# A fused decoder trunk: at the borders between sub-layers, VectorE's low-part split of the first row tile moves in front of the gate products of the second

## The reference

```
h = rmsnorm(x, g_pre) * (1 + scale) + shift      # scale, shift, gate come from a vector c
y = sublayer(h)                                   # products of h with weights
x = x + gate * rmsnorm(y, g_post)
```

## Time and profile before

| | us |
|---|---|
| median of 3 runs (878.6 to 879.68) | 879.16 |
| the profiled execution, its time | 878.76 |
| its span, first to last instruction | 877.0 |
| PE busy | 863.8 (99%) |
| PEld busy | 719.7 (82%) |
| DVE busy | 661.7 (75%) |
| ACT busy | 419.0 (48%) |
| POOL busy | 115.5 (13%) |
| mean granted TensorE clock | 0.991 |

### The profile page before, as it was taken

How to read it: one execution, slowest core, us unless ns; L and a number is a source line. 1 busy time by engine, 2 the same in 40 slices (tenths; PEclk the granted TensorE clock), 3 DMA queues, 4 the chain that set the end, 5 groups by cost and what they waited for, 6 DMA issues and landing times.

```text
span 877.0 us, 11703 instructions
## 1 busy us (share of the span) xinstructions
PE 863.8 (99%) x4259; PEld 719.7 (82%) x4259; DVE 661.7 (75%) x1170; ACT 419.0 (48%) x635; POOL 115.5 (13%) x103
## 2 busy tenths in 40 slices
PE   9999999999999999999999999999999999999996
PEld 8987888888877888888888778888887788888885
DVE  4688989898788676676488899888787855644844
ACT  4464655465545543443336555465554635434521
POOL 1610120301221040300321030030030100000300
PEclk8999999999999999999999999999999999999998
DMA  8886764767344878677445766566644374665511
GB/s 343 355 305 238 241 223 172 285 200 304 104 163 155 350 260 322 251 262 280 171 144 201 280 222 258 193 231 233 255 146 169 104 281 168 237 244 190 206 59 48
DMA packets 34362, 194.09 MB, mean 221 GB/s; under 512 B 4481, under 2 KB 4481, under 8 KB 16770
## 3 DMA queue, kind: packets, MB, share of 16 engines
q1 hardware_dynamic: 32978, 189.64, 58.7%
q0 software_dynamic: 1328, 3.71, 1.3%
HBM read 192.29 MB, written 1.05 MB: 220 GB/s over the span
## 4 chain that ended last, share of the span: by engine, by line
PE 90%; DVE 6%; DMA 2%; issue 1%; ACT 1%; SPq 0%; DVEq 0%; ACTq 0%
PE ps L1232 26%; PE ps L1234 26%; PE ps L1233 25%; PE ps L1283 5%; PE ps L1335 2%; PE ps L1372 2%; DMA wide_t<-ada_first 1%; DVE w_lo L845 1%; PE ps L1363 1%; PE ps L1357 1%; PE ps L1356 1%; PE ps L1355 1%; PE ps L1334 1%; PE ps L1317 1%; DVE pj L1081 1%
## 5 line engine op out<-in xcount | busy, mean ns | idle before, releaser
L845 DVE TENSOR_TENSOR w_lo<-raw,w_hi 128x2048 fp32r<-128x2048 f32 (+1 forms) x132 | 303.8, 2309 | 48.4 <-ACT w_hi L606 46.6
L1232 PE MATMUL ps<-w_hi,t_hi 128*128 128x512 f32 (+1 forms) x832 | 326.7, 393 | 2.0 <-DVE t_lo L1037 1.9
L1234 PE MATMUL ps<-w_hi,t_lo 128*128 128x512 f32 (+1 forms) x832 | 319.8, 384 | 0.0
L1233 PE MATMUL ps<-w_lo,t_hi 128*128 128x512 f32 (+1 forms) x832 | 319.1, 384 | 0.0
L606 ACT ACTIVATE w_hi<-raw 128x2048 fp32r<-128x2048 f32 (+1 forms) x132 | 249.8, 1895 | 13.6 <-PE ps L1234 9.2
L1232 PEld LDWEIGHTS ps<-w_hi,t_hi 128*128 128x128 f32 x832 | 157.3, 189 | 34.8 <-DVE t_lo L1037 3.3
L1234 PEld LDWEIGHTS ps<-w_hi,t_lo 128*128 128x128 f32 x832 | 157.1, 189 | 30.9
L1233 PEld LDWEIGHTS ps<-w_lo,t_hi 128*128 128x128 f32 x832 | 157.5, 189 | 28.5
L499 POOL PARTITION_ALL_REDUCE wide_t<-wide_t x10 | 64.2, 6422 | 586.9 <-DVE wide_t L863 586.9
L863 DVE SCALAR_TENSOR_TENSOR wide_t<-ada,cs,wide_t 128x1024 f32<-128x1024 f32 x80 | 102.3, 1279 | 0.8 <-DMA ada<-w_ada 0.5
L1232 PE MATMUL ps<-w_hi,m_hi 128*128 128x512 f32 x240 | 99.2, 414 | 0.2
(11 more groups left out here) (164 smaller groups left out, 793.7 us busy)
## 6 DMA issues: line engine op xcount, KB each, us to landing
raw<-w_stream SPq DMA_DIRECT2D x128, 1024.0 KB, 5.9
ada<-w_ada SPq DMA_DIRECT2D x80, 512.0 KB, 5.3
wide_t<-ada_first SPq DMA_DIRECT2D x5, 1024.0 KB, 8.4
wide_t<-gains POOLq DMA_DIRECT2D x7, 512.0 KB, 5.2
mixed<-ada_first SPq DMA_DIRECT2D x3, 1024.0 KB, 6.7
raw<-w_stream SPq DMA_DIRECT2D x4, 656.0 KB, 6.4
x<-x_in SPq DMA_DIRECT2D x1, 1024.0 KB, 5.1
out<-x SPq DMA_DIRECT2D x4, 256.0 KB, 2.0
```

Source lines behind the costliest of these rows:

```text
L845: nc.vector.tensor_tensor(w_lo[:, U % RING, 0:n], raw[:, U % RAW, 0:n], w_hi[:, U % RING, 0:n].bitcast(F32), ALU.subtract).then_inc(s_lo, 1)
L1232: nc.tensor.matmul(dst, hi, w_h, start=first, stop=False)
L1233: nc.tensor.matmul(dst, hi, w_l, start=False, stop=False)
L1234: return nc.tensor.matmul(dst, lo, w_h, start=False, stop=last)
```

## The change

In DVE's `border`, `h_lo(to, kind, 0)`, the two low-part subtractions of tile 0, is issued in front of `gated(l, mid, 1)`, the two gate products of tile 1, and no longer behind them. Four instructions at each of three borders change places; nothing is added or removed, and no other engine's program changes.

```diff
                     scaled(0)
                     dve.wait_ge(s_shift, 2 * l + (1 if mid else 2))
                     normed(l, mid, 0)
-                gated(l, mid, 1)
                 if more:
                     h_lo(to, kind, 0)
+                gated(l, mid, 1)
                 added(l, mid, 1)
                 if more:
                     scaled(1)
```

## The result

The changed kernel is slower: 885.08 us median of 13 runs (880.7 to 887.8) against 879.46 for the kernel before (13 runs, 877.68 to 882.65), ratio 1.0055 with a 95% interval of 1.0042 to 1.0069. The forecast was 882.4, a ratio of 1.0037, from +3.26 us. Measured are +5.6 us by the two medians and +4.8 by the ratio: direction right, size too small by 2.4 or 1.6 us. The profiled execution took 881.74 us, span 880.0, mean granted clock 0.995, so it stands near the low end of its kernel. That it is 3.3 us under the median is part of what had to be explained.

A forecast was written before the change was run, and what follows sets the result against it. PE, busy 99% of the span, was taken as the bound. Shifts of 0.97 + 1.33 + 0.96 = 3.26 us took the profiled 878.76 us to 882.02, and 0.40 more to the median gave 882.4 us; range 880.8 to 884.5.

The forecast's parts named there:

- The bound and the mechanism: At the borders: PE bounds the kernel, and tile 1's chain from DVE's `added` to PE has no slack.
- The shifts: Later start of `added(1)` on DVE, reaching PE in full: 0.97 us at A, 1.33 at B, 0.96 at C.
- Tile 0's gain: Border A: `t_lo` of tile 0 starts 0.39 us sooner, PE can use only 0.21, which lengthens its tile 1 wait.
- Border B as the worst one: Border B: gate products sit wholly in DVE's wait for `t_hi`; moving them gains tile 0 nothing and costs +1.33 us.
- The absorbed shift: Later stages: DMA or POOL's reductions set the pace, hiding up to half the shift; about +1.2 us, 880.4; chance 0.12.
- tile 0 decides: Borders A and C: tile 1's transposes are released early enough, only 0.21 us each comes back; -0.4 us, 878.8; chance 0.04.
- reordering: On DVE: gate products run while the subtraction ahead of them waits, so no effect; chance 0.03.
- The clock: PE's 3.2 us between tiles at A and C drops its clock: 884.1 us for one border, 885.7 for both; chance 0.17.
- 0.50 behind A or C: Sign of a wrong prediction: PE's clock rows show 0.50, that is 1.2 and not 2.4 GHz, after border A or C.

The follow-up runs named there:

- with fills: Changed kernel plus useless matmuls in PE's waits around tile 1's transposes at A and C (two of four runs also at B): pooled mean 883.29 us against 884.83.
- the second profile: Profile from a repeat of the changed kernel, word for word the same: 885.47 us median of 7 against 878.92 for the kernel before.
- the pure-delay run: Kernel before, old order, with useless DVE instructions in front of `added(1)`, two at A and C, three at B: 887.11 us median of 6, ratio 1.0096.
- the third profile of the changed kernel: Profile from another repeat of the changed kernel, nothing altered: 884.32 us median of 12 against 880.36 for the kernel before.

## Why the prediction was right, and what was mis-sized

**The bound and the mechanism.** Right. Tile 1's chain from `added(1)` to PE had no slack, and PE's start was moved by all of the delay; the delay alone does it too (+4.09 us of stretch with nothing moved). One piece of the evidence was misread: of the ten waits of weight loads for `normed`, four are tile 0's, the longest (0.73 and 0.71 us) among them; tile 1's six come to 1.5 us, the longest 0.38.

**The shifts.** Predicted 0.97, 1.33 and 0.96, sum 3.26; measured 1.01, 1.41 and 1.01, sum 3.43. The term that was too small is the step from the gate products to `added`: I took 0.04 us from the pair of dependent steps on SBUF, and it is 0.10 (259.41 + 1.28 to 260.79). DVE's idle of 0.72 us at A and the 1.35 us of the two subtractions were right to 0.01.

**Tile 0's gain.** I gave PE 0.21 us, from the bracket of its wait. The real matmuls start 2.89 us after `normed(0)` and not 3.27, so it was 0.38, which is the whole of `t_lo`'s 0.39: the shown end of the fills is later than the moment from which PE could start. As argued, it reached nothing.

**Border B as the worst one.** Right: the gate products lay wholly in a wait, and `t_lo` of tile 0 did not move.

**The absorbed shift, tile 0 decides, reordering.** None occurred; the distances between the stretches are unchanged to 0.13 us.

**The clock.** This is the term that was left out of the sum. I wrote "If it falls, 3.3 us at half speed lose 1.65 us" and gave it 0.17, with the full clock as the likeliest case. The price of a fall was nearly right (1.43 and 1.56 measured); the chance was not. The pooled 1.5 us between the changed kernel without and with fills would be, at 1.5 us a fall, about one in each execution, over two borders. That is an estimate: falls were seen in one profile of three, two of them, and none in the profile of the new order at A and C alone. The rows I had (2.0 us left the clock alone, 3.9 us did not) bracketed the new 3.2 us; seen from the result, about even odds for each border and an added term of some 1.5 us would have come closer: 3.43 + 1.5 gives 4.9, and 5.1 is measured. The prediction also named 0.50 behind A or C as a sign of being wrong; by that sign its clock failed in the second profile, and its chain did not.

**Slower by how much.** 885.08 lies 0.6 us above the upper end of the stated range; the ratio times the given median of before (1.0055 x 879.16 = 884.0) lies inside it, near the end that allowed for one fall of the clock.

What stays open: why the clock falls in one execution and not in another with the same stretch (11.90 and 11.88 us at A), how much of the changed kernel's lower mean clock arises at the borders and how much in the first 60 us by chance, and whether the slow output transfer is in every execution of the pure-delay run.

## What to carry to other kernels

An instruction moved in front of ready work must itself be ready: here it was put ahead of two products that had filled the wait for it, and DVE, whose rows stand in program order, paid that wait in full on whatever came next. Before advancing something on an engine, look whether the consumer's longest wait is for this tile or for the next one; PE waited 0.21 us for the first and 0.75 for the second. And when a change lengthens a stretch in which PE has no large matmuls, price a fall of its clock as a term of the sum, not as an accident; here fills in the wait delayed nothing (a stretch of 11.89 us at A with them, 11.88 without) and took 1.5 us (+-0.5) off.

## What the runs showed of the hardware

Every kernel scatters, the one before included (877.2 to 884.1 us), and in the profiles the differences begin in the first 60 us, where PE's clock falls too. The windows there, of the kernel before and of the third profile of the changed kernel:

```profile
0.00:60.00 60.00, 58.91 (x356) 0.91 0.86 329
```

```profile
0.00:60.00 60.00, 58.57 (x344) 0.86 0.83 317
```

With 0.91 `normed(0)` at A started at 256.27, with 0.86 at 258.97: 2.7 us of difference before the changed code is reached. The clock isn't all of it: in two profiles with 0.94 there that start is 256.01 and 257.03. A comparison of single executions would have been worth little; the stretches inside the traces repeat to 0.03 us.
